# Where the fp32r halves begin in SBUF: gated halves, unshifted early halves and the experts' stationary operands moved by 8 to 64 bytes

## The reference, cut to what matters

```python
def swiglu(h, w13, w2):                       # first block: four times
    a, b = jnp.split(h @ w13, 2, axis=-1)
    return (jax.nn.silu(a) * b) @ w2
...
def swiglu_2(h, w_gate, w_up, w_down):        # second block: once
    return (jax.nn.silu(h @ w_gate) * (h @ w_up)) @ w_down
...
def _conv_ffn(h, w_up, conv_w, conv_b, w_down):   # third block: once, with a 3-tap convolution
...
    return (jax.nn.silu(gate) * val) @ w_down
```

## Time and profile before

| | us |
|---|---|
| median of the three timed runs | 3061.91 |
| the profiled execution's own time | 3071.65 |
| its span (first to last instruction) | 3069.8 |
| TensorE busy with matmuls | 2980.9 (97%), 20659 records |
| TensorE busy with weight loads | 2730.0 (89%) |
| VectorE busy | 2340.9 (76%) |
| ScalarE busy | 1725.5 (56%) |
| HBM read | 735 MB, 240 GB/s over the span |

### The profile page before, as it was taken

The page is one execution under the profiler, slowest core; times in us unless marked ns, Lnnn a source line. Parts: engine busy times, 40 slices in busy tenths (PEclk is TensorE's granted clock), DMA queues, the critical chain, the costliest instruction groups (busy, mean ns, idle before and its releaser), DMA issues.

```text
span 3069.8 us, 48420 instructions
## 1 busy us (share of the span) xinstructions
PE 2980.9 (97%) x20659; PEld 2730.0 (89%) x20659; DVE 2340.9 (76%) x2704; ACT 1725.5 (56%) x1982; POOL 73.7 (2%) x143
## 2 busy tenths in 40 slices
PE   9999999999989999899989999999999999999999
PEld 8999899999979998899987887888888888899999
DVE  6897788888667567655867888888898888766775
ACT  5435344534535445444746776777777777545553
POOL 0110001010000000000000000000000000000000
PEclk9999999999999999999999999999999999999999
DMA  8785478686513653255316998998999899533352
GB/s 338 289 319 202 151 250 307 215 313 246 208 64 147 224 183 111 83 206 193 124 69 260 349 356 329 366 352 337 365 346 368 339 355 365 209 123 133 124 208 108
DMA packets 112381, 739.27 MB, mean 241 GB/s; under 512 B 12480, under 2 KB 12480, under 8 KB 32160
## 3 DMA queue, kind: packets, MB, share of 16 engines
q1 hardware_dynamic: 92304, 662.77, 57.7%
q0 software_dynamic: 19856, 73.34, 6.8%
HBM read 735.01 MB, written 1.05 MB: 240 GB/s over the span
## 4 chain that ended last, share of the span: by engine, by line
PE 77%; DVE 12%; ACT 4%; DMA 4%; issue 2%; SPq 0%; DVEq 0%; POOL 0%; ACTq 0%
PE ps L570 59%; PE ps L569 16%; DVE wlo L2995 4%; DMA ring<-in_w 3%; ACT whi L1997 2%; PE ps L579 2%; DVE cv L2974 2%; DVE AF L2974 1%; DVE T L2965 1%; DVE att L2983 1%; DVE gf L2977 0%; DVE gf L2965 0%; DVE AR L2965 0%; DVE AR L2974 0%; ACT AR L1982 0%
## 5 line engine op out<-in xcount | busy, mean ns | idle before, releaser
L2995 DVE TENSOR_TENSOR wlo<-ring,whi 128x2048 fp32r<-128x2048 f32 x620 | 1415.7, 2289 | 396.1 <-ACT whi L1997 394.4
L1997 ACT ACTIVATE whi<-ring 128x2048 fp32r<-128x2048 f32 x620 | 1184.6, 1915 | 325.4 <-issue 177.9
L570 PE MATMUL ps<-whi,AR 128*128 128x512 f32 (+1 forms) x2884 | 910.4, 392 | 0.3 <-DVE AF L2965 0.3
L570 PEld LDWEIGHTS ps<-whi,AR 128*128 128x128 f32 x2884 | 536.5, 188 | 119.4 <-DVE AF L2965 0.8
L570 PE MATMUL ps<-hh,whi 128*128 128x256 f32 x2272 | 639.1, 281 | 0.7 <-DVE hl L2965 0.6
L570 PE MATMUL ps<-hl,whi 128*128 128x256 f32 x2272 | 631.9, 278 | 0.0
L570 PE MATMUL ps<-hh,wlo 128*128 128x256 f32 x2272 | 631.8, 278 | 0.0
L570 PE MATMUL ps<-wlo,AR 128*128 128x512 f32 (+1 forms) x1442 | 559.8, 388 | 0.0
L570 PEld LDWEIGHTS ps<-hh,whi 128*128 128x128 f32 x2272 | 428.4, 189 | 6.6 <-DVE hl L2965 1.9
L570 PEld LDWEIGHTS ps<-hl,whi 128*128 128x128 f32 x2272 | 427.0, 188 | 1.2 <-issue 1.0
L570 PEld LDWEIGHTS ps<-hh,wlo 128*128 128x128 f32 x2272 | 426.1, 188 | 0.2
(11 more groups left out here) (275 smaller groups left out, 3479.5 us busy)
## 6 DMA issues: line engine op xcount, KB each, us to landing
ring<-in_w SPq DMA_DIRECT2D x620, 1024.0 KB, 5.0
rring<-in_r POOLq DMA_DIRECT2D x135, 512.0 KB, 4.8
first<-in_r SPq DMA_DIRECT2D x8, 512.0 KB, 18.6
ring<-in_r SPq DMA_DIRECT2D x4, 512.0 KB, 8.5
rring<-in_r SPq DMA_DIRECT2D x3, 512.0 KB, 17.4
AF<-in_mem SPq DMA_DIRECT2D x1, 1024.0 KB, 8.1
X<-in_x SPq DMA_DIRECT2D x1, 1024.0 KB, 16.8
AF<-in_cst POOLq DMA_DIRECT2D x1, 1024.0 KB, 5.4
```

Source lines behind the costliest of these rows:

```text
L570: return self.e.matmul(out, l, r, start=start, stop=stop)
L1997: self.e.activation(N.whi[:, c % HB, :], N.ring[:, c % RING, :], ACT.Copy).then_inc(N.sem["hi"], 1)
L2995: self.e.tensor_tensor(N.wlo[:, c % HB, :], N.ring[:, c % RING, :], N.whi[:, c % HB, :].bitcast(F32), ALU.subtract).then_inc(N.sem["lo"], 1)
```

## The change

Four numbers in `lay` change. No instruction is added, taken away or moved: each engine's list is the same, and only the addresses in it differ.

```diff
-        self.f_gh, self.f_gl = zip(*[pair(at) for at in (224, 736, 1248)])
+        self.f_gh, self.f_gl = zip(*[pair(at) for at in (220, 738, 1252)])
...
         ar = Arena(self.AR)
-        ar.n = 3872
+        ar.n = 3878
         self.vh, self.vl = ar.take(8, S), ar.take(8, S)
...
         ar = Arena(self.AR)
+        ar.n = 4
         self.e_Sel = ar.take(2, 2 * P)
         self.o_Sel = ar.take(2, P)
```

## The result

The change made the kernel slower. Five timed runs gave a median of 3076.97 us (3073.16 to 3080.41) where the kernel before has 3061.91 (3058.99 to 3064.67): a ratio of 1.004, with a 95% interval of 1.0025 to 1.0055, or 8 to 17 us. The forecast was 3051. The profiled execution of the changed kernel took 3076.97 us, with a span of 3075.2 us, 5.4 us more than the profiled execution before.

A forecast was written before the change was run, and what follows sets the result against it. TensorE was taken to bound the kernel, a nanosecond per matmul counting in full. Terms -4 (gated halves), -7 (neighbours' rhythm) and three of 0 gave -11 us: 3061.9 to 3051 us; range 3016 to 3086.

The forecast's parts named there:

- Gated halves: First term, feed-forward down steps: 3168 matmuls moved from 64 to 80, 56 and 48 bytes; -4 us taken, bounds -4 to +17.
- The neighbours' rhythm: Second term, feed-forward blocks: down steps restart the rhythm, all slow matmuls on unmoved halves turn fast; -7 us taken, +32 otherwise.
- Early halves: Third term: 384 unshifted early-half matmuls go from 64 to 40 bytes; 0 taken, bounds -2 to +3 us.
- Experts: Fourth term, experts' stretch: 4038 matmuls of 512 columns go from 64 to 80 bytes; 0 taken, bounds -27 to +27 us.
- The rest: Fifth term, gather, selection, output halves and writers: 128 matmuls at most by 7 ns, under 1 us; 0 taken.
- the milder case: Feed-forward blocks: slow rhythm follows only pair 1 and the fast one is found again in other steps; about +20, 3082 us.
- the rival of the lost rhythm: Feed-forward blocks: ragged starts slow gated and early halves and leave up matmuls slow; +42, 3104 us at full size; chance 0.16.
- the signs given for being right: About 1450 records instead of 1392 in ff3's window, 36 in 4 us in six slow steps, three expert matmuls still 0.70 us.
- The sign for the ragged start: Feed-forward blocks: three down matmuls of f = 1, 4, 7, 10 at 0.36 us would show the forecast wrong.

The follow-up runs named there:

- the map: Kernel before with rows of matmuls behind its end, at operand distances of 0 to 248 bytes in steps of 8, a second such run adding finer distances: 3533.05 and 3417.1 us.
- the second profile: The kernel before, unchanged, profiled once more: span 3058.1 us, against 3069.8 in its first profile.
- The scans: Two runs of the kernel before with test matmuls behind its end, the first varying operand distance, the second also moving both operands together: 3533.05 and 3417.1 us.

## Why the prediction was wrong

The bound was read right: TensorE filled every stretch, and each nanosecond on a matmul came out as one on the kernel. The failing step is the first term of the sum, and with it the second: the forecast is about 23 us below the measured change of some +12, of which the first term has 15 to 18 and the second 9 to 13, while the experts' gain of 5 to 9, taken as 0, hides a part.

1. *Gated halves.* The prediction took the lower end, "since 48, 56 and 80 are much nearer to 64 than to 0 or 128". They ran at 119.2, 120.0 and 119.2, mean 119.8, close to the upper end: +11.4 to +13.7 us instead of -4. The argument supposed a rate that changes smoothly with the distance. No row supported that: the rows had one point at 64 and one at 128, and the map has a notch that ends less than 4 bytes to either side of 64 (120.0 at 60 and at 68). The upper end of +17 was in the range and was the better choice from the rows, since both kinds of operand that they had away from 64 (the rows of 258 columns and the gather) were at 120.
2. *The neighbours' rhythm.* That the down steps break the rhythm and start it anew was right, and that ff3 would leave its slow one too. But each distance leaves its own, as ff2 and ff3 show: 80 and 48 leave the fast one, 56 the slow one. Instead of -7 us the class lost 1.8 against the first profile and 6.1 against the second. The 11 us that could be won back (4 and 7 in the first two terms) were moreover in good part an accident of the one profiled execution: in the second profile these two classes had 6.6 us less with no address changed. That execution took 10 us more than the median of the timed runs, and the prediction called this 0.3% of no weight. A good half of it was the very thing that the prediction tried to win back.
3. *Early halves.* 0 taken, +1.5 to +2.0 us measured; within the bounds of -2 to +3.
4. *Experts.* 0 taken, -1.4 ns or -5.7 us measured, within the bounds. The lower end of -27 us does exist, at 120 bytes and not at 80.
5. *The rest.* 0, as taken.

With the measured terms the sum from the second profile is +13.7 + 6.1 - 5.0 + 2.0 = +17. The time lies in the stated range only because that was kept wide for both signs (the forecast's own range was 3044 to 3056), and it is luck in part: the experts' gain, which the sum hadn't, took 5 to 9 us off. The time is near the milder case of the rival of the lost rhythm (3082); but that rival's mechanism, a ragged start, holds only in part. Its pair 1 is indeed the worst, and leaves the slow rhythm behind, yet pairs 0 and 2 begin on a 16-byte place and lost 4.7 ns against the mean of 114.5 all the same. Of the signs given for being right none came: ff3's window went to 1401 records and not to 1450, no down step ran at the 113.3 ns that 36 records in 4 us would have shown, and three expert matmuls took 0.695 us. The sign for the ragged start came, three down matmuls of pair 1 at 0.36 us, but the other two pairs showed it as well.

The Trainium skill (SBUF — State Buffer, "SBUF: two separate sides") holds that TensorE waits on no one there. The scans, with the other compute engines idle, have 113.3 to 129.5 ns for one form by where its two operands lie to each other and by what came before, so the trace doesn't agree, and the measurement decides. No other compute engine was at work to wait for; that TensorE's two read streams hinder each other is the nearest explanation, and no run here tests it by itself.

## What to carry to other kernels

Where TensorE is the bound and each matmul of fp32r loads new weights, the distance between the two operands modulo 256 bytes is worth 6% of its rate (113.3 against 120.0 ns); measure a map of it with a few dozen matmuls per distance, and don't interpolate between two points of it. Let each row of the map run until its intervals repeat: at 144 bytes the first dozen intervals hide a rate as good as the best. A step's rate also depends on what ran before it, so the profile of one execution can show a loss that the next execution hasn't; profile the kernel before twice before a gain is counted on undoing something that one profile shows. Where a profiled execution lies well off the median of the timed ones, look first for what is peculiar to it.

## What the runs showed of the hardware

- 256 columns of fp32r with a new stationary tile each never ran below 113.3 ns when settled, and 512 columns never below 226.6: 17/16 of the columns at 2.4 GHz (106.7 and 213.3 ns). The granted clock was 1.00 in all these windows. What the extra sixteenth is stays open.
- 117.8 and 113.3 ns are two steady states of one instruction stream at a distance of 64 bytes, each kept for 160 us without a break and both found at the same address; transposes between may switch it, and the same code on the same chip had ff2 in the one and in the other.
- At 144 bytes 256 columns settle at 113.3 ns too, after up to a dozen slower matmuls: in eight of nine rows of the scans (the ninth was at 120.0) and in every down step of the two kernels with gated halves there. None of these steps stayed at 117.8, as many do at 64.
- At a distance of 152 bytes one entry gave 129.5 ns for 256 columns (alternately 138 and 122) and the other 119.9; at 248 bytes 120.0 and 126.7.
- Why the map has this form stays open; no run here tests a model of it.
